# One TensorE stream, two norms: the convolution's norm placed inside the last pair of heads

## The reference, cut to what matters

```python
proj = rms_norm(h, norm_mix) @ w_in
y_conv = silu(layer_norm(depthwise_conv(conv_val * sigmoid(conv_gate), 31 taps)) )
y_rwkv = rwkv7_time_mix(r, k, v, w, a, g)          # 16 heads, norm of each head
h = h + concatenate([y_conv, y_rwkv]) @ w_out
h = h + hierarchical_moe(rms_norm(h, norm_ffn))     # 32 experts, 384 MB of weights
```

## Time and profile before

| | us |
|---|---|
| median of 3 runs | 3931.97 |
| range of the runs | 3931.15 to 3932.44 |
| the profiled execution | 3928.38 |
| its span in the trace | 3926.5 |
| PE busy | 3567.9 (91%) |
| DVE busy | 1265.1 (32%) |
| mean granted clock of PE | 0.976 |

### The profile page before, as it was taken

How to read it: one execution, slowest core, us unless ns; L and a number is a source line. 1 busy time by engine, 2 the same in 40 slices (tenths; PEclk the granted TensorE clock), 3 DMA queues, 4 the chain that set the end, 5 groups by cost and what they waited for, 6 DMA issues and landing times. The chain is left out here.

```text
span 3926.5 us, 48039 instructions
## 1 busy us (share of the span) xinstructions
PE 3567.9 (91%) x20349; PEld 2122.4 (54%) x20349; DVE 1265.1 (32%) x2316; ACT 532.4 (14%) x957; POOL 413.4 (11%) x402
## 2 busy tenths in 40 slices
PE   3999999999789897777777777999999999999999
PEld 2355555555534532222223226755446888888888
DVE  2134445556621300000000004426302355454442
ACT  1122121222111100000000003110011010331000
POOL 0000000000000000000000000002020000365511
PEclk9999999999899899999999998999999999999999
DMA  3211121111141399999999987412542322222432
GB/s 94 65 44 46 46 66 45 46 44 46 66 164 54 137 414 422 422 422 422 421 420 420 416 349 184 142 56 89 129 112 92 124 73 83 73 84 97 166 117 77
DMA packets 318636, 666.29 MB, mean 170 GB/s; under 512 B 42924, under 2 KB 227670, under 8 KB 265077
## 3 DMA queue, kind: packets, MB, share of 16 engines
q1 hardware_dynamic: 310645, 636.35, 44.8%
q0 software_dynamic: 7808, 27.28, 1.9%
HBM read 636.44 MB, written 43.91 MB: 173 GB/s over the span
## 5 line engine op out<-in xcount | busy, mean ns | idle before, releaser
L362 PE MATMUL first_bank<-whole_big 128*128 128x512 f32 x1344 | 637.7, 612 | 9.3 <-DMA whole_big<-in_w_in 9.3
L1774 PE MATMUL experts_run_bank<-whole_big 128*64 128x512 f32 x2048 | 492.5, 629 | 168.7 <-DMA whole_big<-in_expert_w_gate 101.8
L2297 PE MATMUL stream_bank<-whole_big 128*128 128x256 f32 x2912 | 639.2, 381 | 0.6 <-DVE whole_big L3399 0.6
L2297 PEld LDWEIGHTS stream_bank<-whole_big 128*128 128x128 f32 x2912 | 553.2, 191 | 79.1 <-issue 3.7
L2202 PE MATMUL stream_bank<-whole_big 128*128 128x512 f32 x1024 | 443.9, 594 | 0.0
L1774 PEld LDWEIGHTS experts_run_bank<-whole_big 128*64 128x64 f32 x2048 | 170.5, 144 | 489.7 <-issue 489.7
L362 PEld LDWEIGHTS first_bank<-whole_big 128*128 128x128 f32 x1344 | 242.3, 191 | 272.8 <-issue 252.7
L2202 PEld LDWEIGHTS stream_bank<-whole_big 128*128 128x128 f32 x1024 | 193.3, 190 | 236.1 <-issue 235.6
L1794 PE MATMUL experts_run_bank<-whole_big 128*64 128x512 f32 x1024 | 229.9, 596 | 35.2 <-DMA whole_big<-in_expert_w_down 22.8
L1839 DVE TENSOR_TENSOR whole_big<-whole_big,experts_run_bank 128x512 f32<-128x512 f32 x16 | 11.0, 688 | 651.0 <-PE experts_run_bank L1774 651.0
L2348 DVE TENSOR_TENSOR whole_big<-stream_bank,whole_big 128x256 f32<-128x256 f32 x250 | 102.1, 422 | 330.2 <-PE stream_bank L2297 330.2
(11 more groups left out here) (467 smaller groups left out, 3160.1 us busy)
## 6 DMA issues: line engine op xcount, KB each, us to landing
whole_big<-in_expert_w_gate SPq DMA_DIRECT2D x128, 1024.0 KB, 27.9
whole_big<-in_expert_w_up SPq DMA_DIRECT2D x128, 1024.0 KB, 29.6
whole_big<-in_expert_w_down SPq DMA_DIRECT2D x128, 1024.0 KB, 26.8
whole_big<-in_w_in SPq DMA_DIRECT2D x110, 1024.0 KB, 7.8
whole_big<-in_w_out SPq DMA_DIRECT2D x16, 1024.0 KB, 7.3
whole_big<-in_w_out SPq DMA_DIRECT2D x8, 2048.0 KB, 13.5
gates_two<-whole_big SPq DMA_DIRECT2D x40, 256.0 KB, 8.1
whole_big<-gates_two POOLq DMA_DIRECT2D x40, 256.0 KB, 3.1
```

The source lines that it names most:

```text
L362: mm = pe.matmul(bank[:, :], slot[:, k, sub * P:(sub + 1) * P], u_T[:, k, :], start=(k == 0), stop=(k == KD - 1))
L1774: mm = pe.matmul(bank[self.half(h), :], self.x_T[:, PARTS * q + k, self.half(h)], self.ring[slot][:, k, :], start=(q == 0 and k == 0), sto ...
L2297: mm = pe.matmul(self.place[m % 3], weights[:, k, :], left[:, k, :], start=(k == 0), stop=(k == self.k - 1))
```

## The change

The order of units in `UNITS_ONE` is new: val 0 joins `FIRST` (ten units, 16 more fillers before pair 0), and gates and values come one pair earlier, so that all convolution tiles are done by the end of pair 6 (pair 1 has two tiles, pair 6 two, pair 7 none). `LAST_SHARE` has 48 fillers instead of 64. Pair 7 has 76 fillers, by `CLOSE_SHARE`: eight products of the sum in A0, eight of the squares' sum in L0 and L0b, then 60 steps of output units from slot L3 on. The norm's DVE and ACT steps are hung on slots (`CONV_CENTRES` and its fellows), with three square buffers, and two banks of `DenseOne` instead of R[0] and R[1]. DVE's adds of output units 0 to 5 are inside pair 7. In the DVE program behind it the last pair's `centre`, `var`, and `flip_y` to `finish_y` stand at output units 7, 10 and 11 (before: ahead of unit 0, and after units 2, 4 and 5). On SP, the loads that waited for the scaling and `sync_early` now stand after panel 23; panel 24 stays last.

```diff
-FIRST = [("lora", 0), ("rank", 0), ("rank", 1), ("r", 0), ("k", 0), ("v", 0), ("v", 1), ("r", 1), ("k", 1)]
-LATER = [("val", 0), ("gate", 0), ("r", 2), ("k", 2), ("val", 1), ("gate", 1), ("v", 2), ("v", 3), ("r", 3), ("k", 3),
...
-         ("r", 7), ("k", 7), ("val", 7), ("gate", 7)]
+FIRST = [("lora", 0), ("rank", 0), ("rank", 1), ("r", 0), ("k", 0), ("v", 0), ("v", 1), ("r", 1), ("k", 1), ("val", 0)]
+LATER = [("gate", 0), ("val", 1), ("gate", 1), ("val", 2), ("r", 2)]
+LATER += [unit for j in range(2, 7) for unit in (("k", j), ("v", j), ("gate", j), ("val", j + 1), ("r", j + 1))]
+LATER += [("k", 7), ("gate", 7), ("v", 7)]
+SUM_U, VAR_U, OUT_U = N_IN, N_IN + 1, N_IN + 2
-LAST_SHARE = (5, 4, 4, 5, 5, 4, 5, 3, 2, 3, 2, 2, 2, 2, 2, 2, 1, 1, 1, 1, 1, 1, 6)
+LAST_SHARE = (5, 4, 4, 4, 4, 3, 4, 4, 3, 2, 2, 1, 1, 1, 1, 1, 2, 2, 0, 0, 0, 0, 0)
+CLOSE_SHARE = (8, 0, 0, 4, 4, 0, 0, 0, 0, 4, 4, 4, 4, 4, 4, 4, 4, 4, 4, 4, 4, 4, 8)
+def out_finished(slot):
+    done = sum(CLOSE_SHARE[:slot]) - 2 * CT
+    return range(max(done, 0) // 8, max(done + CLOSE_SHARE[slot], 0) // 8)
+CONV_CENTRES = {"A1": range(0, 4), "A2": range(4, 8)}
+CONV_SQUARES = {"A1": range(0, 3), "L0": range(3, 8)}
+CONV_VAR, CONV_ROOT, CONV_FLIP = "L0b", "L0b", "L1"
+CONV_SCALES = {"L1b": range(0, 4), "L2": range(4, 8)}
+CONV_SOFT = {"L2": range(0, 4), "L2b": range(4, 8)}
...
-        squares = [kk, k2]
-        conv_var, conv_rstd = rate, e_inv
+        squares = [kk, k2, key_tmp]
+        conv_var, conv_rstd = rate, change
+        out_left = OUT_U + (sum(CLOSE_SHARE) - 2 * CT) // 8
...
-                    if panel == PANELS_IN + 2:
-                        middle.sync_early(sp)
                     if panel == PANELS_IN + 1:
                         sp.wait_ge(dense.product, N_IN)
                         sp.dma_start(rows[:, :, :], a["x"][0].rearrange("(t p) d -> p t d", p=P)).then_inc(sem["rows_in"], 16)
+                    if panel == PANELS_IN + 2:
                         sp.wait_ge(sem["c_scaled"], CT)
+                        sp.wait_ge(sem["y_mm"], CT)
                         middle.sync_late(sp, 0)
                         middle.sync_late(sp, 1)
+                        middle.sync_early(sp)
                 middle.sync(sp)
...
+                def close():
+                    n = closed[0]
+                    closed[0] = n + 1
+                    i = n % CT
+                    if n < CT:
+                        wait("conv", 32 * (n + 1))
+                        if i == 0:
+                            dense.open(pe, SUM_U)
+                        mm = pe.matmul(dense.bank[SUM_U % 2][:, :], ones[:, :], mixed_T[:, i, :], start=(i == 0), stop=(i == CT - 1))
+                        if i == CT - 1:
+                            mm.then_inc(dense.product, 1)
+                    elif n < 2 * CT:
+                        if i == 0:
+                            dense.open(pe, VAR_U)
+                        wait("c_sq", i + 1)
+                        mm = pe.matmul(dense.bank[VAR_U % 2][:, :], ones[:, :], squares[i % 3], start=(i == 0), stop=(i == CT - 1))
+                        mm.then_inc(*((sem["c_var_mm"], 1) if i < CT - 1 else (dense.product, 1)))
+                    else:
+                        if n == 2 * CT:
+                            dense.at = OUT_U
+                            wait("c_done", CT)
+                        dense.out_step(pe, mixed_T)
...
                 dense.fill(pe, u_T, KD)
                 bonus_sum(0)
+                dense.fill(pe, u_T, KD)
                 for j in range(CT):
                     pair(j)
-                wait("conv", 32 * CT)
...
+                close_to(out_left + 1)
                 mean(CT - 1)
-                wait("c_done", CT)
-                for i in range(16):
-                    dense.out_unit(pe, N_IN + i, mixed_T)
-                    if i == 1:
-                        variance(CT - 1)
+                close_to(out_left + 3)
+                variance(CT - 1)
+                close_to(OUT_U + 16)
                 wait("pair_done", CT)
...
-                    tiles = ([], [0], [1], [2], [3], [4], [5, 6], [7])[j]
+                    tiles = ([], [0, 1], [2], [3], [4], [5], [6, 7], [])[j]
...
+                left = out_finished(len(SLOTS_ONE) - 1)[0]
+                for i in range(left, 16):
+                    if i == left + 1:
+                        centre(CT - 1)
+                    if i == left + 4:
                         var(CT - 1)
-                    if i == 4:
+                    if i == left + 5:
                         flip_y(CT - 1)
-                    if i == 5:
                         norm_y(CT - 1)
                         finish_y(CT - 1)
                         middle.vector_early(dve)
+                    add_row(i)
                 middle.vector(dve)
```

More of the change, by code:

```diff
@@ L371, in fill, with open, out_step @@
             self.step(pe, u_T)
-    def out_unit(self, pe, u, mixed_T):
+    def open(self, pe, u):
+        pe.wait_ge(self.bank_free[u % 2], u // 2)
+        return self.bank[u % 2]
+    def out_step(self, pe, mixed_T):
+        u, k = self.at, self.k
         panel = panel_of_one(u)
-        slot, use, token = self.ring[panel % 2], panel // 2, (u - N_IN) % 4
+        slot, use, token = self.ring[panel % 2], panel // 2, (u - OUT_U) % 4
         wide = slot[:, :, :].rearrange("p (k two) c -> p k (two c)", two=2)
         bank = self.bank[u % 2]
[L379 to L384, removed]
+        if k == 0:
+            self.open(pe, u)
+        if token == 0 and k % 4 == 0:
+            pe.wait_ge(self.arrived[panel % 2][k // 4], 16 * use + 16)
+        mm = pe.matmul(bank[:, :], mixed_T[:, k, token * P:(token + 1) * P], wide[:, k, :], start=(k == 0), stop=(k == 7))
+        self.k += 1
+        if self.k == 8:
+            mm.then_inc(self.product, 1)
+            self.at, self.k = u + 1, 0
     def freed(self, eng, u):
@@ L510, in _ @@
                     dense.load(sp, panel)
[L511 removed]
+                    if nearest < CT and panel < PANELS_IN and dense.last(panel - 2) >= len(FIRST) + 5 * (nearest - 2) + 2:
                         load_up(nearest)
                         nearest += 1
[L514 to L515 removed]
                     if panel == PANELS_IN + 1:
@@ L606, in fill @@
                         spent[name] = spent.get(name, 0) + n
-                        dense.fill(pe, u_T, n)
+                        if more:
+                            dense.fill(pe, u_T, n)
+                        else:
+                            for _ in range(n):
+                                close()
                     def settle(mm, name):
@@ L751, in _, with close_to @@
                 bonus_sum(0)
+                dense.fill(pe, u_T, KD)
                 for j in range(CT):
                     pair(j)
-                wait("conv", 32 * CT)
[L755 to L763, removed]
-                mean(CT - 1)
-                wait("c_done", CT)
-                for i in range(16):
-                    dense.out_unit(pe, N_IN + i, mixed_T)
-                    if i == 1:
-                        variance(CT - 1)
+                def close_to(u):
+                    while dense.at < u:
+                        close()
+                close_to(out_left + 1)
+                mean(CT - 1)
+                close_to(out_left + 3)
+                variance(CT - 1)
+                close_to(OUT_U + 16)
                 wait("pair_done", CT)
@@ L855, in units @@
                             evict(u)
+                        if not more and name in CONV_SQUARES:
+                            for i in CONV_SQUARES[name]:
+                                square_conv(i)
+                        if not more and name in CONV_SOFT:
+                            for i in CONV_SOFT[name]:
+                                soft_conv(i)
+                        if not more and name == CONV_ROOT:
+                            root_conv()
                     units("A0")
@@ L928, in _ @@
                 evict(8)
+                evict(9)
                 for j in range(CT):
                     pair(j)
[L931 to L938, removed]
-                    wait("c_scaled", i + 1)
-                    act.activation(mixed_T[:, i, :], mixed_T[:, i, :], ACT.Silu, bias=cols["conv_ln_b"][:, i:i + 1],
-                                   scale=cols["conv_ln_g"][:, i:i + 1]).then_inc(sem["c_done"], 1)
                 square_y(CT - 1)
@@ L1135, in rest @@
                                 n -= now
+                        if more:
+                            return
+                        if i:
+                            for u in out_finished(i - 1):
+                                add_row(u)
+                        for k in CONV_CENTRES.get(name, ()):
+                            centre_conv(k)
+                        if name == CONV_VAR:
+                            var_conv()
+                        if name == CONV_FLIP:
+                            flip_conv()
```

(4 more changed lines are left out.)

78 lines of the change are left out of this document (47 added, 31 removed).

## The result

The changed kernel takes 3943.42 us (median of 7 runs, 3941.99 to 3946.15) against 3931.37 us for the kernel before in the same rounds. The ratio is 1.0034, with a 95% interval of 1.0022 to 1.0046: slower, by 12 us. The forecast was 3949.4, the range 3937 to 3962. The profiled span is 3941.4 us, 14.9 more than before.

The account below looks back on a forecast made before the run. The prediction took PE to bound most of the first layer's stream, with loss to win from 1007.8 to 1098.8 us. Terms +13.8 - 5.6 - 20.1 + 27.2 + 2.1 = +17.4 on 3931.97 gave 3949.4 us, range 3937 to 3962.

Parts of the forecast that it names:

- PE's later start of pair 0, from one unit more: Prologue: sixteen more fillers run ahead of pair 0 with nothing to hide them, +13.8 us.
- pair 6 gives back: Pair 6: 16 fillers fewer return only 5.6 of the 13.8 us, since DVE is nearly solid there.
- PE's wait before level 2: Pair 7's first half: PE waits 6.6 us for DVE, which does the norm in series.
- first output product after pair 7's start: Pair 7: the first output product starts 50 us after the pair does, range +46 to +53.
- unit 11's end after pair 7's start: Output units behind pair 7: PE stays full and unit 11 ends 156.3 us after the pair's start.
- pair 7 to the last output unit, change without stall: From pair 7's start to the last output unit: 20.1 us saved before counting the stall.
- stall: Ahead of output unit 12: PE waits 27.2 us for panel 24, queued on SP behind router weights and seven chunks.
- low clock behind it: Output units after the stall: PE runs at the low clock once more, +2.1 us.
- price in proportion: After the stall: a low-clock cost growing with idle time would make the sum 3 to 4 us higher.
- overtaking panel: Rival at unit 12: panel 24 lands ahead of the chunks, stall 15.7 us, total 3937.9 us; chance 0.09.
- case without a stall: Rival at unit 12: the last pair's values come early enough, the 11.9 us gain stays, 3920 us; chance 0.05.
- DVE bounding more than thought: Rival in pairs 6 and 7: pair 6 returns nothing, first output product at +56, 3961 us; chance 0.14.

Follow-up runs that it names:

- e3: Kernel before, with SP issuing panel 24 ahead of the block that waits for the last pair's values and loads expert chunks; 3932.36 us, ratio 1.0003.
- e5: e1 with pair 6's flip_y, norm_y and finish_y on DVE moved behind level 3 in pair 7; 3907.16 us, ratio 0.9943.
- e9: e7 with ScalarE doing the last four Silu of pair 7 ahead of its copy of X; 3904.72 us, ratio 0.9934.
- e1: Changed kernel, with SP issuing panel 24 ahead of the block that waits for the last pair's values and loads router weights and chunks; 3912.32 us, ratio 0.9957.
- e2: Changed kernel, with the seven expert chunks issued behind panel 24, SP's wait and router weights still ahead of it; 3927.27 us, ratio 0.9990.
- e4: Changed kernel, SP's order unchanged, with the last pair's variance and the norm steps behind it done sooner, behind add 8; 3930.88 us, ratio 0.9999.
- e1b: The same kernel as e1, run again in the rounds of e9; 3912.08 us, ratio 0.9955.
- e7: e5 with ten of pair 6's 64 taps also moved from behind L2b to slots up to L2; 3906.37 us, ratio 0.9943.

## Why the prediction was right, point by point

**The result lies in the range and on the forecast side**, with the mechanism named: a wait of about 27 us for `w_out` ahead of the 97th output product. The prediction's own steps:

| step | forecast us | measured us |
|---|---|---|
| PE's later start of pair 0, from one unit more | 13.8 | 10.3 |
| pairs 1 to 5 | 0 to 1 | 0.2 |
| pair 6 gives back | 5.6 | 6.1 |
| PE's wait before level 2 | 6.6 | 6.28 |
| first output product after pair 7's start | 50 | 51.4 |
| unit 11's end after pair 7's start | 156.3 | 155.7 |
| DVE ready to SP, before unit 11's end | 0.2 | 0.3 |
| pair 7 to the last output unit, change without stall | -20.1 | -20.7 |
| stall | 27.2 | 27.35 |
| low clock behind it | 2.1 | 2.3 |
| last output unit, change | +17.4 | +13.2 |

**Prologue: right in the mean, off in this pair of profiles.** The sixteen fillers did cost 13.9 us (32 records at 205.29, below). But the profile of before spent longer at the low clock in its prologue, and its first product came 1.1 us later: 64 records in 30.78 us instead of 30.16, 32 in 15.70 instead of 14.00. That is 3.4 us. The last products of pair 0 began at 310.48 to 314.61 us in two profiles of kernels with nine units ahead of it, and at 324.63 to 328.37 in ten profiles of kernels with ten. The two means are 13.4 us apart, close to the 13.8 of the prediction, but a difference of two single profiles has an error of about 4 us from this stage alone. The difference of the medians, 12.0 us, isn't explained closer than that. The prologue in PE's timeline of the kernel before:

```profile
72.76 30.78 PE L362 MATMUL first_bank<-whole_big 128*128 128x512 f32 x64 [9.35 <-DMA whole_big<-in_w_in]
...
177.71 15.70 PE L362 MATMUL first_bank<-whole_big 128*128 128x512 f32 x32
```

And of the changed kernel:

```profile
71.67 30.16 PE L375 MATMUL first_bank<-whole_big 128*128 128x512 f32 x64 [9.13 <-DMA whole_big<-in_w_in]
...
176.00 14.00 PE L375 MATMUL first_bank<-whole_big 128*128 128x512 f32 x32
...
205.29 13.89 PE L375 MATMUL first_bank<-whole_big 128*128 128x512 f32 x32
219.11 1.15 PE L581 MATMUL first_bank<-whole_big 64*64 64x64 f32 x32
```

**Pair 6.** The step was right in its parts: the state chain is bound by DVE. In the timeline of DVE from 975.34 to 1010.6 there is no idle time at all, where the kernel before had 1.36 us, and PE waits 3.78 us for one advance behind v 7's mix (L783, above). That 6.1 us came back where 5.6 were forecast is in part luck: in the profile of e3, whose code for pair 6 is that of the kernel before, the pair took 6.2 us longer (last section), and against that profile 12.3 would have come back. Against e3 the changed kernel's last output unit ends 10.5 us later, against the kernel before 13.2; the medians' 12.0 lies between.

**Pair 7's halves.** For the first output product +50 was taken against the worked +51 and +46; +51.4 was it, low clock included. That unit 11 still ended at +155.7, where +156.3 was forecast, is in part luck, since the errors nearly cancel. The prediction took pair 0's end as 324.35, a full pair of 115.56 us behind its start; but pair 0 has no sums for an earlier pair's norm, and pair 1 begins at 322.64, so the second half's own work was put 1.7 us too high. And the first output products lost 1.4 us to the low clock, not 2.1. The line of pair 1's start, from PE's timeline of the kernel before:

```profile
322.64 1.15 PE L556 MATMUL first_bank<-whole_big 64*64 64x64 f32 x32
```

e5 and e9 show that the order of work on DVE and ScalarE sets the first half: each edit shortened the wait that it was aimed at, though neither took it off whole.

**The stall.** Every link held: program order on SP, the values ready only after add 10, the chunks ahead of the panel. e1 takes the whole path away, e2 its bytes, e4 shifts its start, e3 shows that it takes the overlap to expose it. One part of the length was not what the prediction read. In the kernel before, the panel was issued at 1156.94, as output unit 7 ended and freed its ring slot, 10.6 us after SP's first issue, and its first half took 16.8 us; in the changed kernel it was issued after 8.1 us and took 19.4. The sum is the same because the seven chunks and the first half, 8 MB, took 23.1 us in the one and 23.2 in the other from the first chunk's issue (1150.57 and 1171.90): the bytes ahead of it set the landing, not the panel's own issue.

**The low clock behind the stall.** It cost 2.3 us behind the 27.35 us of idleness, 2.8 behind e4's 14.30, 2.4 behind e2's 9.99 and 2.1 behind the 10.48 of the kernel before. It doesn't grow with the stall, so the price in proportion, which the prediction set beside its own, falls.

**Rivals.** The overtaking panel (a stall of 15.7) fell with the landings of 19.4 and 21.6 us. A case without a stall, forecast at 3920 with a gain of 11.9 us, was made by e1, by another way than the rival named: its last output unit ends 18.8 us sooner than in the kernel before. The sum was too high by 3.8 us in the prologue (the spread described above), by the 2.1 us of low clock at the first output products, which e1's profile doesn't have (eight records in 3.70 us), and by the 1.7 us of pair 0's end; e1's first output product at +50.5 gives 0.5 back. DVE bounding more than thought fell, since pair 6 gave back its 6 us and the first output product came at +51.4, not +56.

**What isn't settled.** Behind the last output unit the profiles of before and after differ by 1.7 us (2714.8 and 2716.5 to the end). Over the twelve profiles that rest lies between 2712.9 and 2717.0, and e1 and e1b, which are the same kernel, are 3.3 us apart there (2716.6 and 2713.3). So 1.7 us is within what two profiles of one kernel differ by.

## What to carry to other kernels

When work is moved forward on one engine, list every transfer that it will want and look at what its queue issues ahead of it: a wait in a DMA queue's program order cost nothing here as long as the consumer was late, and its length, with all bytes issued ahead of the wanted load, once the consumer was early. Put the load with the nearest due time in front of bulk prefetches, even where the present timing hides the order. And once fillers thin out, the engine that was half idle on average (DVE, 356 of 702 us over pairs 0 to 5) can bound a stretch of 20 us: place its optional work in the slots where it waits, not evenly.

## What the runs showed of the hardware

**A DVE operation took longer beside a GpSimd product.** In e5 a scaling of 128x512 from SBUF took 1.76 us, where the one before and the two behind it took 0.68, while GpSimd's own product ran (1.66 us instead of its usual 1.27). e7 and e9, with the same order, show the same: four scalings in 3.56 us and a GpSimd product of 1.66. In the changed kernel, where DVE did a reciprocal at that moment, GpSimd took 1.26 and the four scalings behind it 2.43. The kernel before has it too: a tap at 362.20 took 1.71 us instead of 0.75 beside GpSimd's product at 362.10, which there took its usual 1.27. DVE's timeline of e5:

```profile
1049.71 1.76 DVE L1012 TENSOR_TENSOR whole_big<-whole_big 128x512 f32<-128x512 f32 x1
```

and GpSimd's timeline of e5, with the usual product first:

```profile
1043.32 1.27 POOL L1378 TENSOR_TENSOR whole_big<-whole_big 128x512 f32<-128x512 f32 x1 [10.77 <-PE first_bank L597]
1049.26 1.66 POOL L1378 TENSOR_TENSOR whole_big<-whole_big 128x512 f32<-128x512 f32 x1 [4.67 <-PE first_bank L597]
```

**The low clock varies between executions of the same code.** From 984 to 1008, around DVE's chain in pair 6, the kernel before was granted 0.86 of the full clock; e3, which has the same instructions and is some 4 us ahead in them, got 0.64, and from the last product of pair 5 to pair 7's start took 121.6 us instead of 115.4. What differs is where the low clock fell. In both, PE waited four times for DVE's advances, and these came at the same distances (the two last waits end at 992.41 and 995.13 in the kernel before, at 988.28 and 991.00 in e3). In the kernel before the fillers ran slow from 989.96 to 997.4, mostly while PE would have waited for DVE anyhow, so its two last waits are only 0.67 and 0.24 us long:

```profile
989.96 1.79 PE L362 MATMUL first_bank<-whole_big 128*128 128x512 f32 x2
992.41 0.48 PE L727 MATMUL first_bank<-whole_big 64*64 64x64 f32 x4 [0.67 <-DVE whole_big L1117]
992.82 2.08 PE L362 MATMUL first_bank<-whole_big 128*128 128x512 f32 x2
995.13 0.48 PE L727 MATMUL first_bank<-whole_big 64*64 64x64 f32 x4 [0.24 <-DVE whole_big L1117]
```

In e3 the clock stayed full up to the last wait and was low behind it, from 991.0 to about 1007 (0.57 granted from 991.0 to 1009.9), where PE had no wait to hide it:

```profile
988.28 0.33 PE L726 MATMUL first_bank<-whole_big 64*64 64x64 f32 x4 [1.33 <-DVE whole_big L1116]
988.54 1.13 PE L362 MATMUL first_bank<-whole_big 128*128 128x512 f32 x2
991.00 0.48 PE L726 MATMUL first_bank<-whole_big 64*64 64x64 f32 x4 [1.34 <-DVE whole_big L1116]
991.41 2.07 PE L362 MATMUL first_bank<-whole_big 128*128 128x512 f32 x2
```

So the longer waits of e3 are a consequence of its full clock ahead of them, not the cause of the low one. Why the clock fell at different points isn't settled. The windows of e3 (columns as in the earlier trace rows):

```profile
990.00:1000.00 10.00, 9.00 (x50) 4.13 (x52) 8.59 (x16) 0.00 (x0) 0.00 (x0) 0.50 0.01 2
1000.00:1010.00 10.00, 10.00 (x72) 5.59 (x72) 0.00 (x0) 1.88 (x2) 0.00 (x0) 0.64 0.00 0
```

The fillers of that stretch ran at about half speed (2.07 us instead of 1.13 for two records), that is 1.2 GHz. The Trainium skill, TensorE: Matmul & The Clock Gate, "What's actually happening", knows just two levels, 1.2 and 2.4 GHz; the 0.50 of the first window agrees with the lower, and the 0.64 is a mean over both. A profile of one execution can't price a stretch with small holes in PE closer than some 6 us.
